# Cache attention loop: value products half a step later, two rope packings moved into the prompt stage

## What is computed

```python
c_past = cache_latent[l][page_table].reshape(Bs, -1, KV_LORA)      # 8 x 4096 x 256
kpe_past = cache_krope[l][page_table].reshape(Bs, -1, MLA_D_ROPE)  # 8 x 4096 x 32
...
s = jnp.einsum('bqhc,bkc->bhqk', q_lat, c) + jnp.einsum('bqhr,bkr->bhqk', q_pe, k_pe)
p = jax.nn.softmax(jnp.concatenate([s_past, s_new], axis=-1), axis=-1)
return jnp.einsum('bhqk,bkc->bqhc', p[..., :P], c_past) + ...
```

## Time and profile before

| | us |
|---|---|
| median of 3 runs | 1118.54 (1118.19 to 1119.13) |
| profiled execution | 1116.36 |
| its span | 1114.6 |
| TensorE busy in it | 1022.3 (92%) |
| mean granted TensorE clock | 0.962 of full speed |
| VectorE, ScalarE, GpSimd busy | 540.0, 430.1, 164.2 |

### The profile page before, as it was taken

The page is one execution under the profiler, slowest core; times in us unless marked ns, Lnnn a source line. Parts: engine busy times, 40 slices in busy tenths (PEclk is TensorE's granted clock), DMA queues, the critical chain, the costliest instruction groups (busy, mean ns, idle before and its releaser), DMA issues.

```text
span 1114.6 us, 20673 instructions
## 1 busy us (share of the span) xinstructions
PE 1022.3 (92%) x8636; PEld 865.4 (78%) x8636; DVE 540.0 (48%) x1084; ACT 430.1 (39%) x873; POOL 164.2 (15%) x258
## 2 busy tenths in 40 slices
PE   3999999999977878889898979999999999999997
PEld 3989889777745534555555559999999999999997
DVE  5555857564478349634443453264334334433433
ACT  6444755655331446433333342353124113213412
POOL 1021300465320200235344100000000000000000
PEclk9999889999589899989999989999999999999999
DMA  6312110300011600256665232132222232232212
GB/s 228 100 58 79 46 33 34 115 5 5 1 37 36 225 21 1 66 191 217 209 229 201 82 114 77 39 133 76 86 104 76 81 109 77 79 111 76 77 39 81
DMA packets 24999, 101.76 MB, mean 91 GB/s; under 512 B 7752, under 2 KB 8568, under 8 KB 18435
## 3 DMA queue, kind: packets, MB, share of 16 engines
q1 hardware_dynamic: 15690, 62.68, 16.8%
q0 software_dynamic: 9216, 37.75, 9.7%
HBM read 96.21 MB, written 4.22 MB: 90 GB/s over the span
## 4 chain that ended last, share of the span: by engine, by line
PE 61%; DVE 8%; ACT 3%; issue 2%; POOL 1%; ACTq 0%; DVEq 0%
PE PS L567 13%; PE PS L565 13%; PE PS L566 13%; PE PS L1008 4%; PE PS L1043 3%; PE PS L1019 2%; PE PS L897 2%; PE PS L1026 2%; ACT PE L1512 1%; DVE SMX L1985 1%; PE PS L1034 1%; PE PS L924 1%; ACT PTE L1525 1%; PE PS L943 1%; POOL CN L2192 1%
## 5 line engine op out<-in xcount | busy, mean ns | idle before, releaser
L565 PE MATMUL PS<-XH,WH 128*128 128x272 f32 (+1 forms) x944 | 277.2, 294 | 3.2 <-DVE WL L1589 1.7
L567 PE MATMUL PS<-XH,WL 128*128 128x272 f32 (+1 forms) x944 | 276.1, 292 | 0.0
L566 PE MATMUL PS<-XL,WH 128*128 128x272 f32 (+1 forms) x944 | 275.2, 292 | 0.0
L565 PEld LDWEIGHTS PS<-XH,WH 128*128 128x128 f32 x944 | 180.1, 191 | 8.3 <-issue 4.2
L566 PEld LDWEIGHTS PS<-XL,WH 128*128 128x128 f32 x944 | 180.2, 191 | 0.0
L567 PEld LDWEIGHTS PS<-XH,WL 128*128 128x128 f32 x944 | 179.9, 191 | 0.0
L1152 ACT ACTIVATE WH<-RAW 128x2048 fp32r<-128x2048 f32 x47 | 89.9, 1913 | 203.9 <-PE PS L567 202.7
L565 PE MATMUL PS<-NH,WH 128*128 128x272 f32 x512 | 149.1, 291 | 0.8 <-DVE WL L1589 0.8
L567 PE MATMUL PS<-NH,WL 128*128 128x272 f32 x512 | 147.6, 288 | 0.0
L566 PE MATMUL PS<-NL,WH 128*128 128x272 f32 x512 | 146.6, 286 | 0.0
L1589 DVE TENSOR_TENSOR WL<-RAW,WH 128x2048 fp32r<-128x2048 f32 x47 | 108.0, 2297 | 63.4 <-ACT WH L1152 63.4
(11 more groups left out here) (313 smaller groups left out, 1518.5 us busy)
## 6 DMA issues: line engine op xcount, KB each, us to landing
RAW<-in_w_stream SPq DMA_DIRECT2D x47, 1024.0 KB, 4.9
XN<-in_hin SPq DMA_DIRECT2D x4, 512.0 KB, 6.7
out_y_p<-YO SPq DMA_DIRECT2D x4, 512.0 KB, 2.7
WQ<-in_wq SPq DMA_DIRECT2D x1, 1536.0 KB, 8.1
CST<-in_big SPq DMA_DIRECT2D x1, 1132.5 KB, 13.3
SS<-in_sstate SPq DMA_DIRECT2D x1, 1024.0 KB, 4.8
out_ssm_s<-SS SPq DMA_DIRECT2D x4, 256.0 KB
CN<-in_cache,IDX POOLq DMA_INDIRECT x64, 6.1
```

Source lines behind the costliest of these rows:

```text
L565: pe.matmul(PS[:, b, 0:n], wh, xh[:, k, c:c + n], start=(k == 0), stop=False)
L566: pe.matmul(PS[:, b, 0:n], wh, xl[:, k, c:c + n], start=False, stop=False)
L567: last = pe.matmul(PS[:, b, 0:n], wl, xh[:, k, c:c + n], start=False, stop=(k == DT - 1))
```

## The change

Nothing is computed otherwise; instructions are put in another order.

- TensorE: the value products of step n - 2 stand behind transposes u 3 of step n (they were those of n - 1 behind u 8). The probability transposes of n - 1 stand behind u 8 (before: behind u 6). The loop has an 18th turn for the values of step 15.
- ScalarE: the copy into `PTE` stands behind the copy of u 8 (before: behind that of u 7).
- VectorE: `accumulate(n - 2)` stands behind the copy of u 4, with an 18th turn (before: `accumulate(n - 1)` at the step's end).
- GpSimd: the packing is a function, `pack_rope(n)`. Steps 0 and 1 are packed right behind gathers 0 and 1, ahead of the wait for `pv_done` and ahead of gathers 2 and 3. From step 3 on a gather stands ahead of the packing of the step: gather(n + 1) waits for the values of n - 3, then step n is packed (before: step n packed, then gather(n + 3) behind the values of n - 1).

```diff
 TensorE
-            for n in range(17):
+            for n in range(18):
                 for u in range(9):
                     if n < 16:
                         cache_transposes(n, u)
-                    if n >= 1 and u == 1:
+                    if 1 <= n <= 16 and u == 1:
                         cache_scores(n - 1, 1)
                         cache_rope_scores(n - 1)
+                    if n >= 2 and u == 3:
+                        cache_values(n - 2)
                     if n < 16 and u == 5:
                         cache_scores(n, 0)
-                    if n >= 1 and u == 6:
+                    if 1 <= n <= 16 and u == 8:
                         cache_p(n - 1)
-                    if n >= 1 and u == 8:
-                        cache_values(n - 1)
 ScalarE
-                    if n >= 1 and u == 7:
+                    if n >= 1 and u == 8:
                         act.wait_ge(sem("ce_pt"), n)
 VectorE
-            for n in range(17):
+            for n in range(18):
                 for u in range(9):
                     if n < 16 and u in CT_DVE:
                         cache_copy(n, u)
-                    if n >= 1 and u == 3:
+                    if 1 <= n <= 16 and u == 3:
                         cache_max(n - 1)
-                    if n >= 1 and u == 8:
-                        accumulate(n - 1)
+                    if n >= 2 and u == 5:
+                        accumulate(n - 2)
 GpSimd
-            pool.wait_ge(sem("pv_done"), NT_)
-            gather(2)
-            gather(3)
-            for n in range(16):
+            def pack_rope(n):
                 if n >= 2:
                     pool.wait_ge(sem("ct_mm"), 9 * (n - 1))
                 pool.wait_ge(sem(f"cn_in{n % 4}"), 64 * (n // 4 + 1))
                 for b in range(4):
                     last = pool.tensor_copy(KRN[n % 2][:, :, b, :], CN[n % 4][b][:, :, KV:KV + DR])
                 last.then_inc(sem("kr_packed"), 1)
-                if 1 <= n < 13:
-                    pool.wait_ge(sem("ce_pv"), n)
-                    gather(n + 3)
+            pack_rope(0)
+            pack_rope(1)
+            pool.wait_ge(sem("pv_done"), NT_)
+            gather(2)
+            gather(3)
+            for n in range(2, 16):
+                if n >= 3 and n + 1 < 16:
+                    pool.wait_ge(sem("ce_pv"), n - 2)
+                    gather(n + 1)
+                pack_rope(n)
```

## The result

The changed kernel takes **1087.31 us** (median of five runs, 1075.41 to 1089.16), the kernel before 1118.54 (1110.63 to 1119.13): ratio 0.9727, 95% interval 0.9685 to 0.9769. The forecast was 1090.5 with a range of 1085 to 1098.

The account below looks back on a forecast made before the run. The prediction took the cache stage to be bound by TensorE's own order of work plus waits. Gains of 11.1 (start), 16.9 (steps) and 0 (end), together 28.0 us, off 1118.54 gave 1090.5 us, range 1085 to 1098.

Parts of the forecast that it names:

- The stops of a step: TensorE's waits ahead of probability transposes (0.56 us) and value products (0.97 us) both vanish, with nothing late next.
- The slack of the exponential: In a step, ScalarE's exponential ends at 6.75 us, 2.5 us before the probability transposes need it.
- The length of a step: Fourteen even steps: 9.70 us each, between 9.57 and 9.85, where 10.93 was measured; gain 16.9 us.
- Rival (b): Steps: TensorE's busy time stays and each semaphore wait leaves a 0.17 us gap; 10.2 per step, 1097.5 us; chance 0.12.
- The gathers: In the steps, gathers first issued 6.32 us into a step take 10.6 us to land, leaving 2.5 us to spare.
- (c): Steps: gathers land late and set the step; at 14 us latency a step is 10.2, time 1097; chance 0.08.
- (d): Steps: late gathers cost more than everything gained; at 20 us latency a step is 13.2, time 1139; chance 0.03.
- GpSimd's pace: In the gather loop, GpSimd's issue instruction keeps its 933 to 1163 ns, median 937, priced unchanged.
- The start: Steps 0 and 1: early packing gains 11.1 us through the wait, later values, step 1's stops and the clock.
- the clock at 1.00 from the stage's start on: At the start, TensorE does not go to the lower clock, worth about 1.8 us of the gain.
- The tail: Stage end: values 14 are hidden behind step 15's rope scores; gain taken as 0, bounds -0.2 to +1.3 us.
- The base: Whole kernel: 28.0 us taken off the median 1118.54, which stands 2.2 above the profiled execution's 1116.36.

Follow-up runs that it names:

- the experiment: Changed kernel with the probability transposes put back behind u6 and ScalarE's copy behind u7, the value products staying moved: 1079.8 us (one execution).
- The two late-gather runs: Changed kernel with each gather held to the end of its step's transposes, or to u2 of the next step: 1101.81 us and 1179.84 us.
- the repetition: The changed kernel itself measured once more, nothing altered: 1088.03 us, ratio 0.9763.
- the packing alone: Kernel before, with only the packing of steps 0 and 1 moved ahead of the wait for the prompt's values: 1109.87 us, ratio 0.9951.

## Why the prediction was right, step by step

- **The stops of a step.** Right: both go, and none comes elsewhere. The prediction took the two moves together and did not say which of them removes which stop; the experiment shows that the values' move alone removes both. The slack of the exponential already held the reason: the 2.5 us to spare were mostly the values in between.
- **The length of a step.** The mis-sized term. 9.70 was taken between 9.57 and 9.85; measured 9.58, so fourteen steps gave 18.4 us, not 16.9. The reading of starts was right (9.40 and one cut of 0.17), and u8 to probabilities costs none: 486.73 to 487.17 is 0.44, both being transposes. The upper end came from the busy time, 9.85, whose modelled ends of products overlap the next ones; starts of loads were the better ruler, and the middle needed no room for it. Rival (b), 10.2, falls with that.
- **The gathers.** Right, and near its own numbers. The first issue comes 2.24 us behind the load of the values in the same step (484.27 against 482.03); from a first issue to the packing it takes 10.56 us (GpSimd's timeline, last gather), against 10.6:

```profile
580.07 0.96 POOL L2192 DMA_INDIRECT CN<-in_cache,IDX  x1 [3.89 <-PE PS L1043]
...
590.63 1.03 POOL L2208 COPY KRN<-CN 128x128 f32<-128x128 f32 x4 [4.87 <-DMA CN<-in_cache,IDX]
```

  The issue is 6.24 us into the step (484.27 against its first transposes' load at 478.03). With steps of 9.58 that leaves 2 x 9.58 - 6.24 - 10.56 = 2.4 us to spare. Rivals (c) and (d) didn't come to pass. The two late-gather runs show that their mechanism is real. The formula gave the mean step where the loss was small (10.4 and 10.42); where it was large it was too low (14.7 and some 17), since late copies and a falling clock come on top, and (d) was priced too low with it.
- **GpSimd's pace.** The issue instruction kept its 933/937/1163 ns (source view of L2192 in after), so the starvation of GpSimd that the Trainium skill, page "SBUF — State Buffer", section "SBUF: two separate sides", describes was not seen; no row tells whether an instruction of this loop is in a two-port mode, so the rule itself was not tested. What was seen in its place goes the other way: VectorE's and ScalarE's copies are late while GpSimd issues and packs. I had looked for a cost on the one engine alone. In the changed kernel it cost nothing in the steps: there the copies that are due in this time are on time. At the start it can cost some 4 us, with the fall of the clock behind it (18.71 - 12.59, less the 1.7 of the slow first transposes).
- **The start.** 11.2 us against 11.1 in the profiled execution, and 5.1 in the repetition. The wait, the values and the stops went as said. The term that does not hold is the last one, the clock at 1.00 from the stage's start on. I had written that 1.8 would be lost if it fell. It was low in the profile of every experiment, and in the repetition the late copy came beside it, which I hadn't foreseen. That the profiled execution gave 11.2 is to this extent luck.
- **The tail.** I took 0 within -0.2 to +1.3 and 1.5 was measured. The clock was up, 1.93 against 3.21 for the last values, and the waits around them shrank a little. That the filled gap is what keeps it up is likely but not shown, as the packing alone kept it up with the gap empty. What lies behind paid 0.5 us at most: from the last values to the end it is 463.0 us in after and 462.5 in before.
- **The base.** The forecast was set against the median, 1118.54, and the term for the profiled execution against 1116.36. The profiled execution of before has the low stretch ahead of the stage, worth 10.3 us against that of after; whether the executions behind the medians have it, no trace shows. The sum over the changed stage alone kept it out. The forecast of 28.0 us fell 3.2 short of the 31.2 between the medians. In the profiled execution that is what the steps (1.5) and the tail (1.5) gave above their terms. But with the start of the repetition the stage gives 25.0, and 28.0 lies between the two, so that the number came out near owes something to chance.

## What to carry to other kernels

When two stops in a loop hang on one chain of other engines, one larger piece of work set between its ends may cover both; price the new order from starts to starts, with a gap where the form changes and none where it doesn't. A loop that waits for a prefetch has a period of at least (issue position + latency) / steps ahead, and the issue's position also decides which copies of other engines come late, so both are to be worked out before it is moved. Compare stages, not spans: here 10 us between two profiles lay in code that neither version touched.

## What the runs showed of the hardware

- A copy that waits for TensorE can start 1 to 2.4 us late while GpSimd issues a row of indirect DMAs and packs behind them: on VectorE 1.85 us behind the load instead of 0.75 in steady steps and 3.05 in a burst of eight, on ScalarE at 527.54 instead of 525.4. The late copies of ScalarE started 0.02 to 0.15 us behind the end of the packing in 33 steps. Which copies are hit moves with GpSimd's work. Why is open.
- TensorE's clock can stand at its lower level though the engine is busy: 10.00 of 10.00 us busy at 0.50 around 292 us of before, and 0.59 from 458 to 459 us in the repetition. It can also stay up over a gap: 1.00 behind 2.52 us without a product in the packing alone, where behind a gap of the same length in before the last values ran 3.21 us.
- An operation of VectorE with both inputs in SBUF is slower beside GpSimd's packing. The source view of L2030, before and after (ns, min/median/max):

```profile
L2030 DVE TENSOR_TENSOR SME<-SME,ML x16: 158/284/670, 484.1 to 645.8; 128x1 f32<-128x1 f32 x16
```
```profile
L2030 DVE TENSOR_TENSOR SME<-SME,ML x16: 158/159/160, 465.9 to 605.7; 128x1 f32<-128x1 f32 x16
```

  Before, this operation ran into the packing (560.85 to 561.13, the packing from 560.98 on); after, the maximum comes some 2 us behind the packing's end. The Trainium skill, page "SBUF — State Buffer", section "SBUF: two separate sides", names this case, a shared port pair that one of the two engines, whichever starts first, holds for a whole instruction. The trace agrees that the operation becomes longer (a median of 284 ns against 159). It does not bear out who is held: by the rows VectorE's operation starts 0.13 us ahead of the packing and is yet the one that is lengthened, but spans of GpSimd are rough. The rule would not explain the late copies, which have one input, in PSUM.
